# One PSUM bank moved from the turned probabilities to the sum of value products in an attention kernel

## The reference, cut to what matters

```python
def gqa_attend(q, k, v):                      # group A: 8 heads of 64
    s = jnp.einsum('bkgqd,bknd->bkgqn', q, k) * (HEAD_DIM ** -0.5)
    p = jax.nn.softmax(s.astype(jnp.float32), axis=-1).astype(v.dtype)
    return jnp.einsum('bkgqn,bknd->bkgqd', p, v)

def diff_attend(q, k, v, lam):                # group B: 4 heads, two softmax maps each
    s = jnp.einsum('bhjqd,bhjnd->bhjqn', q, k) * (HEAD_DIM ** -0.5)
    p = jax.nn.softmax(s.astype(jnp.float32), axis=-1)
    a = (p[:, :, 0] - lam * p[:, :, 1]).astype(v.dtype)
    return jnp.einsum('bhqn,bhnv->bhqv', a, v)
```

## Time and profile before

| what | value |
| --- | --- |
| median of 3 runs | 2082.66 us (2076.31 to 2084.02) |
| span of the profiled execution | 2084.2 us |
| PE matmul busy | 1818.6 us, 87% of the span |
| PE weight load busy | 1556.0 us, 75% |
| DVE busy | 1218.3 us, 58% |
| ACT busy | 828.5 us, 40% |
| POOL busy | 630.4 us, 30% |
| mean granted clock of PE | 0.929 of full speed |

### The profile page before, as it was taken

One profiled execution on the slowest core, in us unless ns is written; L12 is line 12 of the kernel. 1 busy time (PEld: TensorE's weight loads), 2 busy tenths in 40 slices (PEclk: granted clock), 3 DMA queues, 4 the chain that ended last, 5 costly groups with the idle time before them and its releaser, 6 DMA issues.

```text
span 2084.2 us, 26369 instructions
## 1 busy us (share of the span) xinstructions
PE 1818.6 (87%) x9456; PEld 1556.0 (75%) x9456; DVE 1218.3 (58%) x2125; ACT 828.5 (40%) x1452; POOL 630.4 (30%) x324
## 2 busy tenths in 40 slices
PE   5877987786896998999999978799886889999997
PEld 1776777674685887888888868778775668888886
DVE  2765757656558688755415665576566466335255
ACT  3345664545423333133213334465555334334242
POOL 1123532212111333422322322252322124444442
PEclk9988999896897999999999989799996889999999
DMA  8210013000142223333324331100100123232332
GB/s 327 85 45 8 1 57 106 20 21 1 61 152 71 99 95 139 123 130 121 101 81 130 122 117 54 38 1 16 51 21 21 51 71 101 93 99 91 101 100 82
DMA packets 45166, 166.94 MB, mean 80 GB/s; under 512 B 4752, under 2 KB 4752, under 8 KB 43920
## 3 DMA queue, kind: packets, MB, share of 16 engines
q1 hardware_dynamic: 41696, 156.25, 22.2%
q10 hardware_dynamic: 3376, 9.44, 1.2%
HBM read 161.48 MB, written 4.19 MB: 79 GB/s over the span
## 4 chain that ended last, share of the span: by engine, by line
PE 67%; DVE 16%; issue 9%; ACT 5%; DMA 2%; DVEq 0%; SPq 0%; POOL 0%; ACTq 0%
PE ps L736 19%; PE ps L737 18%; PE ps L738 18%; DVE nb L1636 2%; PE ps L834 2%; DVE ada_junk L1339 2%; PE ps L835 2%; PE ps L755 2%; PE ps L845 2%; DVE pt_lo L1613 1%; PE ps L933 1%; PE ps L720 1%; ACT qk L1085 1%; DMA w_raw<-w_d 1%; DVE p_sb L1605 1%
## 5 line engine op out<-in xcount | busy, mean ns | idle before, releaser
L667 POOL TENSOR_TENSOR w_lo<-w_raw,w_hi 128x1024 fp32r<-128x1024 f32 (+1 forms) x200 | 474.1, 2374 | 1195.0 <-ACT w_hi L1007 1195.0
L736 PE MATMUL ps<-h_hi,w_hi 128*128 128x512 f32 (+1 forms) x1056 | 376.2, 356 | 5.9 <-DVE h_lo L1427 5.9
L737 PE MATMUL ps<-h_lo,w_hi 128*128 128x512 f32 (+1 forms) x1056 | 376.0, 356 | 0.0
L738 PE MATMUL ps<-h_hi,w_lo 128*128 128x512 f32 (+1 forms) x1056 | 375.2, 355 | 0.0
L1007 ACT ACTIVATE w_hi<-w_raw 128x1024 fp32r<-128x1024 f32 (+1 forms) x200 | 201.3, 1007 | 360.5 <-PE ps L738 236.5
L736 PEld LDWEIGHTS ps<-h_hi,w_hi 128*128 128x128 f32 x1056 | 201.0, 190 | 34.8 <-issue 6.4
L698 POOL TENSOR_TENSOR p_sb<-p_sb,ri 128x768 f32<-128x768 f32 (+1 forms) x120 | 156.1, 1307 | 233.3 <-DVE p_sb L1605 126.6
L737 PEld LDWEIGHTS ps<-h_lo,w_hi 128*128 128x128 f32 x1056 | 201.1, 190 | 28.0
L738 PEld LDWEIGHTS ps<-h_hi,w_lo 128*128 128x128 f32 x1056 | 200.8, 190 | 28.1
L736 PE MATMUL ps<-w_hi,h_hi 128*128 128x384 f32 (+1 forms) x560 | 191.0, 341 | 17.2 <-DVE h_lo L1427 12.4
L1636 DVE TENSOR_REDUCE nb<-ps 128x1 f32<-128x768 f32 (+1 forms) x160 | 135.1, 847 | 111.7 <-PE ps L835 111.4
(11 more groups left out here) (133 smaller groups left out, 3315.4 us busy)
## 6 DMA issues: line engine op xcount, KB each, us to landing
w_raw<-w_d SPq DMA_DIRECT2D x152, 512.0 KB, 3.5
ada_b<-ada_d SPq DMA_DIRECT2D x64, 512.0 KB, 3.6
w_raw<-w_d SPq DMA_DIRECT2D x48, 384.0 KB, 3.1
ada_first<-first_d SPq DMA_DIRECT2D x4, 2048.0 KB, 19.7
ada_first<-ada_d SPq DMA_DIRECT2D x4, 1024.0 KB, 11.5
x_sb<-x_d SPq DMA_DIRECT2D x1, 3072.0 KB, 12.1
x_sb<-x_d ACTq DMA_DIRECT2D x1, 3072.0 KB, 10.3
c_bc<-cc_d SPq DMA_DIRECT2D x2, 1024.0 KB, 8.8
```

The costliest lines, as they stand in the source:

```text
L667: nc.gpsimd.tensor_tensor(w_lo[:, c % RING, 0:n], w_raw[:, c % RAW, 0:n], w_hi[:, c % RING, 0:n].bitcast(f32), ALU.subtract).then_inc(w_lo ...
L736: nc.tensor.matmul(out, lh, rh, start=first, stop=False)
L737: nc.tensor.matmul(out, lh, rl_, start=False, stop=False)
L738: return nc.tensor.matmul(out, ll, rh, start=False, stop=last)
```

## The change

`TURNS` goes from 3 to 2. With it go the third PSUM bank of the T steps (bank 6) and the third pair `pt_hi`/`pt_lo` in SBUF (it lay in a region of its own that nothing else gains). Bank 6 now takes the sum of V of even items, bank 7 of odd ones, and the first V of an item waits for the copy to `o_sb` of the item before the last.

```diff
-TURNS = 3
+TURNS = 2
...
-                        x["buf"] = x["tid"] % (2 if p == 1 else TURNS)
+                        x["buf"] = x["tid"] % TURNS
...
-    pt_at = [R_X + 27 * KB, R_X + 31 * KB, R_TAB]
+    pt_at = [R_X + 27 * KB, R_X + 31 * KB]
...
-                        if j == 0 and it["id"] >= 1:
-                            pe.wait_ge(o_done, it["id"])
+                        if j == 0 and it["id"] >= 2:
+                            pe.wait_ge(o_done, it["id"] - 1)
...
-                        mm = three(ps[:, 7, 0:nq], (v_hi[:, s["kt"], vc], v_lo[:, s["kt"], vc]),
+                        mm = three(ps[:, 6 + it["id"] % 2, 0:nq], (v_hi[:, s["kt"], vc], v_lo[:, s["kt"], vc]),
...
-                            A(o_sb[r, it["h"] // 2, it["t0"]:it["t1"]], ps[r, 7, 0:nq], ACT.Copy).then_inc(o_done, 1)
+                            A(o_sb[r, it["h"] // 2, it["t0"]:it["t1"]], ps[r, 6 + it["id"] % 2, 0:nq], ACT.Copy).then_inc(o_done, 1)
...
-                            A(o_sb[:, 4 + 2 * (p - 1) + it["h"], it["t0"]:it["t1"]], ps[:, 7, 0:nq], ACT.Copy) \
+                            A(o_sb[:, 4 + 2 * (p - 1) + it["h"], it["t0"]:it["t1"]], ps[:, 6 + it["id"] % 2, 0:nq], ACT.Copy) \
```

## The result

The changed kernel takes 2130.8 us (median of 4 runs, 2127.69 to 2135.14) where the kernel before took 2082.4 beside it (4 runs): a ratio of 1.0227, 95% interval 1.0210 to 1.0245. The prediction was 2124, with a range of 2107 to 2140. The span of the profiled execution goes from 2084.2 to 2129.3 us, +45.1.

The account below looks back on a forecast made before the run. PE, busiest by far, bounds attention through a ring of T, ACT copy, DVE low half and V. 31.4 + 4.8 + 4.8 + 0 = 41.0 us takes the span from 2084.2 to 2125.2, run median 2124 us; range 2107 to 2140.

Parts of the forecast that it names:

- The second bank, cost 0: First V of each item no longer waits for the previous sum's copy: worth nothing, bounds 0 and -7.8 us.
- The rule that spoke for it: Skill's advice to rotate independent matmul groups through PSUM banks; applied to V sums, it would bring up to 7.8 us.
- the faster rival: V's waits really end with the copy to `o_sb`, and two T buffers suffice: 2075 us, chance 3%.
- Items of p = 0, 16 x 1.96 = 31.4 us: Two T banks and two pairs lengthen each of 16 latent items in p = 0 by 1.96 us; bounds 14.7 to 42.6.
- with banks alone cut each item would lose 0.45: Side estimate for p = 0: cutting T banks but keeping SBUF pairs costs about 0.45 us an item.
- The third pair in p = 2, 4.8 us: Losing the third pair in p = 2, priced from p = 1 against p = 2: 4.8 us, bounds 3.7 to 7.3.
- Two banks in p = 1 and p = 2, 4.8 us: T now comes behind V's wait: 0.6 us for each of 8 latent items, 4.8 us, bounds 3.6 to 7.2.
- The sum, 41.0: Whole kernel: 31.4 + 4.8 + 4.8 + 0 = 41.0 us added to the profiled span of 2084.2 us.
- The signs: Expected in trace: p = 0 latent items 13.0 us, T waiting for `pt_lo`, copies for V, context items unchanged.
- The third pair alone costs 1 us an item: Rival: a p = 0 item costs 1.0 us, not 1.96, as p = 1 against p = 2 shows: 2108 us, 14%.
- The clock falls too: Rival: PE's gaps in p = 0 lower its clock, 0.70 us more an item: 2136 to 2140 us, 12%.
- No change: Rival: items have slack, T3's copy is off the chain and V3 doesn't follow its low half: 2083 to 2092 us, 4%.

Follow-up runs that it names:

- run 1: Changed kernel, but all V sums in bank 7 and the first V waiting for the previous item's copy again: 2132.7 us, ratio 1.0226.
- run 2: Changed kernel with three `pt_hi`/`pt_lo` pairs again in p = 0 and p = 2, T banks still cut: 2097.7 us, ratio 1.0062.
- run 8: Changed kernel with the third `pt_hi`/`pt_lo` pair back in p = 2 alone: 2113.5 us, ratio 1.0164.
- run 3: Kernel before, three T banks and one sum bank kept, with two `pt_hi`/`pt_lo` pairs in all phases: 2118.1 us, ratio 1.0154.
- run 9: Changed kernel with the third `pt_hi`/`pt_lo` pair back in p = 0 alone: 2097.7 us, ratio 1.0084.
- run 4: Changed kernel, with VectorE making a T's low half ahead of the last S step's inverse and subtraction: 2102.9 us, ratio 1.0087.

## Why the prediction was right

**The second bank, cost 0:** right (run 1). The rule that spoke for it, and the faster rival, rested on seven waits in the earlier trace rows; the same rows stand in the kernel after, where V0 no longer waits for that copy.

**Items of p = 0, 16 x 1.96 = 31.4 us:** right, by a chain worked out from one item's timeline. The item grew by 1.94 us, the phases by 32.4 and, in the second profiles, 30.6. The last item of each phase, for which 1.96 was taken without a row, grew by 1.83 and 1.65 (V5 to V5). V5 is 2.41 behind V3 (2.3 forecast). The step "with banks alone cut each item would lose 0.45" was measured at 0.47 (run 2).

**The third pair in p = 2, 4.8 us:** a little small. Run 8 has 5.5 and run 3, with three T banks, 5.6, within the bounds of 3.7 to 7.3. The difference of p = 1 and p = 2 was near the right price there.

**Two banks in p = 1 and p = 2, 4.8 us:** right as far as it can be read. Run 2 has 3.4 + 2.8 = 6.2, within 3.6 to 7.2, and run 8 has 2.7 in p = 2. But p = 1 has the same buffers in seven profiles of the table (the kernel after and run 9, each twice, and runs 1, 2 and 8) and takes 60.1 to 62.9 us in them, so its part is anything from 0.6 to 3.4, where 2.4 was forecast. At equal clock in layer 1 it is 1.1 us (24.8 against 23.7, clock 1.00) and 1.4 (25.6 against 24.2, 0.93), 1.2 forecast. In p = 2 the kernel after grew by 8.2 to 10.4 us in all, 7.2 forecast; of the difference 1.3 us are in layer 0, where the clock was 0.82 and not 0.94, and 0.9 in layer 1 at the same mean clock.

**The sum, 41.0:** attention grew by 44.7 and 41.8 us in two profiles, so of the 7 us by which 2124 lies under the measured 2130.8, the terms of the sum hold 1 to 4. The runs stand at 48.4 us, 4 to 7 more than the phases account for; with the length outside attention varying by 10 us between executions this remainder is not told from scatter, and stays open. One part of it can be placed: in the other executions on record the time is 1.6 to 2.0 us above the span, so the profiled execution of the kernel before (span 2084.2) took, by estimate, about 2086 us, 3 to 4 above the median of its runs, and the spans differ by 45.1 only. The prediction's step from the span to the median, 1.5 us down, passed over this; it does not touch the difference of 41.0.

**The signs.** ACT's copies wait for V, T steps for `pt_lo`, and context items stay as they were: from the first to the last V of those in p = 0 it is 19.05 us before and 19.04 after. The second item of p = 2 grew by 1.8 us in layer 1, within the 1.5 to 2.5 forecast, and in layer 0 by 3.7 at the fallen clock and 2.6 in the second profiles.

**The rivals.** "The third pair alone costs 1 us an item" was wrong for the reason given against it: in p = 0 the pair costs 1.50 an item (run 3) with three banks and (225.3 - 200.5)/16 = 1.55 with two (run 9 against the kernel after; 1.44 against its second profile). That in p = 0 the late copy holds exponentials that nothing else had made late is seen in run 3 (1.07 ahead of L1597) and borne out by run 4. "The clock falls too" did not happen in p = 0: PE went from 41.68 busy of 43.98 us to 42.37 of 51.76, with idle gaps of up to 0.8 us, and the granted clock stayed 1.00; over the whole of p = 0 in layer 0 it was 0.97 before and 0.98 after. By the rival's own terms its time would have been 2138 to 2140, not 2136 to 2140. On this the Trainium skill, "TensorE: Matmul & The Clock Gate", section "A second HAM failure mode: psum-queue depth-cycling", made it likelier; the trace shows no swing in these four items, at pauses of up to 0.8 us. "No change" was excluded by the very number it named: V3 follows its low half. What the prediction did not see is how much of the loss was the order of VectorE's queue (run 4), although its own chain passed through it ("low half queued behind them").

## What to carry to other kernels

Count buffers along the whole ring and price the one whose late release holds up work queued behind the waiting instruction: here a bank for the sums was worth 0, a bank for the turned tiles 13 us, and an SBUF pair 34 us (14 and 29 by the attention phases). When a buffer seems too few, look first at what stands ahead of its release in an in-order queue; moving one operation took the cost from 48 to 25 us, or from 42 to 45 down to 27 by the attention phases, without a byte. And a constant that sizes two things (`TURNS`) should be split before either is judged.

## What was not expected

- A row that names a releaser can be a coincidence that survives the removal of the wait: for the copies to `o_sb` it was 3.2 us in three waits and 4.6 in four before, 3.2 and 4.5 after, when V0 wrote elsewhere.
- PE idled 18% of the time in four items of p = 0 (busy 42.37 of 51.76 us) and kept a granted clock of 1.00, while phase p = 2 of layer 0, idle for a quarter of its length, had 0.82 in one execution and 0.94 in the next.
- The same program spent 1770 and 1782 us outside attention in two executions on two chips, with PE's wait for `a_lo` at 2.0 and 8.7 us.
